# Attention scores in one transformer layer: cross terms over the whole array, high by high terms as pairs of 64-row tiles

## The reference

```python
def diff_attn_block(q, k, v, lam):
    s = jnp.einsum('bqhnd,bkhnd->bnhqk', q, k).astype(jnp.float32) * (1.0 / math.sqrt(HEAD_DIM))
    a = jax.nn.softmax(s, axis=-1)
    a = a[:, 0] - lam * a[:, 1]
    return jnp.einsum('bhqk,bkhv->bqhv', a.astype(v.dtype), v)
```

## Time and profile before

| what | us |
|---|---|
| median of 3 runs (3261.56 to 3263.18) | 3262.38 |
| the profiled execution, its own time | 3265.1 |
| its span, from first to last instruction | 3263.4 |
| TensorE busy in the span | 3125.3 |
| VectorE busy | 2255.1 |
| ScalarE busy | 1595.0 |

### The profile page before, as it was taken

The page is one execution under the profiler, slowest core; times in us unless marked ns, Lnnn a source line. Parts: engine busy times, 40 slices in busy tenths (PEclk is TensorE's granted clock), DMA queues, the critical chain, the costliest instruction groups (busy, mean ns, idle before and its releaser), DMA issues. The chain is left out here.

```text
span 3263.4 us, 67299 instructions
## 1 busy us (share of the span) xinstructions
PE 3125.3 (96%) x22654; PEld 2843.7 (87%) x22654; DVE 2255.1 (69%) x3873; ACT 1595.0 (49%) x3504; POOL 691.6 (21%) x894
## 2 busy tenths in 40 slices
PE   6999999999999999998989985999999999999998
PEld 4988989989998998997878874999999989998997
DVE  4888878878888888887974446555555555555564
ACT  4556656656666666665741123333333433333332
POOL 2532333333333233331310001111111111111111
PEclk8999999999999999999999986999999999999999
DMA  8654344344334345434325543655655555655664
GB/s 289 241 197 125 126 139 131 120 134 139 125 119 152 120 125 154 126 119 149 115 94 213 193 168 129 195 188 189 200 185 181 181 181 191 196 181 183 199 198 119
DMA packets 341095, 530.90 MB, mean 163 GB/s; under 512 B 29658, under 2 KB 256218, under 8 KB 325722
## 3 DMA queue, kind: packets, MB, share of 16 engines
q1 hardware_dynamic: 331228, 494.52, 46.4%
q0 software_dynamic: 9728, 34.61, 4.2%
HBM read 439.10 MB, written 89.16 MB: 162 GB/s over the span
## 5 line engine op out<-in xcount | busy, mean ns | idle before, releaser
L2749 PE MATMUL ps_gu<-xT,e_w 128*128 128x272 f32 x6144 | 782.9, 290 | 2.1 <-DVE xT L2909 2.1
L2749 PEld LDWEIGHTS ps_gu<-xT,e_w 128*128 128x128 f32 x6144 | 778.8, 189 | 4.0 <-issue 2.3
L2898 DVE TENSOR_TENSOR e_w<-e_raw,e_w 128x2048 fp32r<-128x2048 f32 x190 | 435.1, 2290 | 308.0 <-ACT e_w L2802 308.0
L1182 ACT ACTIVATE e<-ps_s,negm 128x1024 f32<-128x1024 f32 (+2 forms) x416 | 473.9, 1144 | 240.7 <-DVE negm L1583 200.2
L1568 DVE TENSOR_REDUCE mx<-ps_s 128x1 f32<-128x1024 f32 (+3 forms) x428 | 526.4, 1233 | 66.1 <-PE ps_s L821 62.0
L821 PE MATMUL ps_s<-kT,qT 128*128 128x512 f32 (+1 forms) x1920 | 478.5, 387 | 14.2 <-ACT e L1182 13.2
L2802 ACT CAST e_w<-e_raw 128x2048 fp32r<-128x2048 f32 x190 | 361.7, 1904 | 187.6 <-PE ps_d L2731 121.2
L821 PEld LDWEIGHTS ps_s<-kT,qT 128*128 128x128 f32 x1920 | 342.8, 191 | 85.8 <-ACT e L1182 28.7
L895 PE MATMUL ps_m<-w,hT 128*128 128x384 f32 x2040 | 392.4, 341 | 3.9 <-DVE o L1635 3.9
L863 PE MATMUL ps_m<-v,aT 128*128 128x128 f32 x2816 | 370.2, 279 | 1.3 <-ACT aT L1166 1.3
L895 PEld LDWEIGHTS ps_m<-w,hT 128*128 128x128 f32 x2040 | 349.7, 189 | 5.4 <-issue 5.4
(11 more groups left out here) (374 smaller groups left out, 3962.7 us busy)
## 6 DMA issues: line engine op xcount, KB each, us to landing
hT<-hT_d SPq DMA_DIRECT2D x85, 1024.0 KB, 5.4
e_raw<-w_gate SPq DMA_DIRECT2D x64, 1024.0 KB, 5.2
e_raw<-w_up SPq DMA_DIRECT2D x64, 1024.0 KB, 7.5
e_raw<-w_down SPq DMA_DIRECT2D x64, 1024.0 KB, 5.0
tab<-tabs_d SPq DMA_DIRECT2D x85, 256.0 KB, 2.7
hT_d<-hT SPq DMA_DIRECT2D x17, 1024.0 KB, 3.9
w_lent<-w_ada SPq DMA_DIRECT2D x16, 1024.0 KB, 5.5
cat_d<-cat_h SPq DMA_DIRECT2D x102, 128.0 KB, 4.7
```

What stands on the lines that cost most here:

```text
L1182: nc.scalar.activation(out, src, ACT.Exp, bias=negm[:, s.par, c:c + 1], scale=HD ** -0.5, accum_out=acc).then_inc(exp_done.sem, 1)
L2749: mm = nc.tensor.matmul(ps_gu[:, 2 * (s % 2) + f, 0:SLOTS], w_view(s, a)[:, k, f * P:f * P + P], xT[:, b, k, :], start=(k == 0 and a + b = ...
L2898: nc.vector.tensor_tensor(w[:, s % RING, 1, :], raw[:, s % RAW, :], w[:, s % RING, 0, :].bitcast(F32), ALU.subtract).then_inc(w_lo, 1)
```

## The change

Each unit of 1024 keys keeps its two banks of 512 columns but is computed otherwise. The key tiles (128 keys) of a unit alternate: even ones have the high parts in the upper 64 rows, odd ones now have the low parts there. The first bank holds the four even tiles, the second the four odd ones, so the moving operand is four runs of 128 columns. For each bank one matmul over the whole array makes both cross terms (half 1 for even tiles, half 0 for odd ones), and one matmul on 64 rows makes high by high: rows 0 to 63 for the first bank, rows 64 to 127 for the second. The low by low product is left out. The last 256 keys are computed as before. Since the columns of the scores are now in another order, `weighted` picks the value tiles through KEY_TILE. On swapped steps (tiles 2, 4, ... 14) `split_kq` and `low_kq` each become two instructions of half the width, and so do the copies of the cached keys. `turn(s, 0)` now stands ahead of the two 64-row matmuls of group 1.

```diff
+    KEY_TILE = [8 * (b // 8) + (2 * (b % 8) if b % 8 < 4 else 2 * (b % 8) - 7) if b < NS else b for b in range(BLOCKS)]
...
+        def swapped(s):
+
+            ref = s.i if s.j is None else s.first + s.odd
+            return 0 < ref < NS and ref % 2 == 0
...
+            def group_scores(s, c, n, lo, hi):
+
+                keys = kT[:, (s.h - 1) % 2, c]
+                q = [qT[:, s.par, (2 * half + c) * P:(2 * half + c + 1) * P] for half in range(2)]
+                paired = hi - lo >= 1024
+                if paired:
+                    tiles = keys[:, lo:lo + 1024].rearrange("p (b o n) -> p b o n", o=2, n=P)
+                    for odd in range(2):
+                        nc.tensor.matmul(ps_s[:, lo + 512 * odd:lo + 512 * odd + 512], q[1 - odd], tiles[:, :, odd, :],
+                                         start=True, stop=False)
+                if hi == KEYS:
+                    if paired and c == 0 and s.back == "prompt":
+                        weighted(s, 0)
+                    for half in range(2):
+                        mm = nc.tensor.matmul(ps_s[:, 2048:KEYS], q[half], keys[:, 2048:KEYS], start=(half == 0), stop=(half == 1))
+                if c == 0 and n == 1 and s.back == "sample" and not late(s):
+                    turn(s, 0)
+                if paired:
+                    for odd in range(2):
+                        rows = slice(64 * odd, 64 * odd + 64)
+                        mm = nc.tensor.matmul(ps_s[:, lo + 512 * odd:lo + 512 * odd + 512], q[odd][rows],
+                                              tiles[rows, :, odd, :], start=False, stop=True)
+                return mm
...
-                        for half in range(2):
-                            lhs = stationary[:, (2 * half + c) * P:(2 * half + c + 1) * P]
-                            for x in range(first, last, 512):
-                                y = min(x + 512, last)
-                                if c == 0 and n == 1 and half == 1 and x == first + 512 and s.back == "sample" and not late(s):
-                                    turn(s, 0)
-                                keys = kT[:, head % 2, c, x:y] if s.front == "sample" else kTp[:, head % 2, c, :]
-                                mm = nc.tensor.matmul(ps_s[:, at + x - lo:at + y - lo], lhs, keys, start=(half == 0),
-                                                      stop=(half == 1))
+                    else:
+                        mm = group_scores(s, c, n, lo, hi)
...
-                    vals = v[:, head % 2, b, :] if s.back == "sample" else vp[:, head % 2, :]
+                    vals = v[:, head % 2, KEY_TILE[b], :] if s.back == "sample" else vp[:, head % 2, :]
...
-                nc.scalar.copy(parts[:, :, 0, :].bitcast(F32R), rot[:]).then_inc(hi_done.sem, 1)
+                if swapped(s):
+                    nc.scalar.copy(parts[:, 0:2, 0, :].bitcast(F32R), rot[:, 0:2, :])
+                    nc.scalar.copy(parts[:, 2:4, 1, :].bitcast(F32R), rot[:, 2:4, :]).then_inc(hi_done.sem, 1)
+                else:
+                    nc.scalar.copy(parts[:, :, 0, :].bitcast(F32R), rot[:]).then_inc(hi_done.sem, 1)
...
-                nc.scalar.copy(past_parts[:, :, :, 0, :].bitcast(F32R), past[:]).then_inc(past_hi, 1)
+                nc.scalar.copy(past_parts[:, 0, :, 0, :].bitcast(F32R), past[:, 0])
+                nc.scalar.copy(past_parts[:, 1, :, 1, :].bitcast(F32R), past[:, 1]).then_inc(past_hi, 1)
...
+                if swapped(s):
+                    nc.gpsimd.tensor_tensor(parts[:, 0:2, 1, :].bitcast(F32R), rot[:, 0:2, :], parts[:, 0:2, 0, :], ALU.subtract)
+                    nc.gpsimd.tensor_tensor(parts[:, 2:4, 0, :].bitcast(F32R), rot[:, 2:4, :], parts[:, 2:4, 1, :],
+                                            ALU.subtract).then_inc(lo_done.sem, 1)
```

More of the change, by code:

```diff
@@ L805, in scores @@
                         weighted(s, 0)
[L806 to L813, removed]
-                        for half in range(2):
-                            lhs = stationary[:, (2 * half + c) * P:(2 * half + c + 1) * P]
-                            for x in range(first, last, 512):
-                                y = min(x + 512, last)
-                                if c == 0 and n == 1 and half == 1 and x == first + 512 and s.back == "sample" and not late(s):
-                                    turn(s, 0)
-                                keys = kT[:, head % 2, c, x:y] if s.front == "sample" else kTp[:, head % 2, c, :]
-                                mm = nc.tensor.matmul(ps_s[:, at + x - lo:at + y - lo], lhs, keys, start=(half == 0),
-                                                      stop=(half == 1))
+                    if s.front == "prompt":
+                        for half in range(2):
+                            q = qTp[:, head % 2, (2 * half + c) * P:(2 * half + c + 1) * P]
+                            mm = nc.tensor.matmul(ps_s[:, 1024 * c:1024 * c + P], q, kTp[:, head % 2, c, :], start=(half == 0),
+                                                  stop=(half == 1))
+                    else:
+                        mm = group_scores(s, c, n, lo, hi)
                     mm.then_inc(s_ready.sem, 1)
@@ L1460, in low_kq @@
                 kq_ready.wait(pool, s)
-                nc.gpsimd.tensor_tensor(parts[:, :, 1, :].bitcast(F32R), rot[:], parts[:, :, 0, :],
-                                        ALU.subtract).then_inc(lo_done.sem, 1)
+                if swapped(s):
+                    nc.gpsimd.tensor_tensor(parts[:, 0:2, 1, :].bitcast(F32R), rot[:, 0:2, :], parts[:, 0:2, 0, :], ALU.subtract)
+                    nc.gpsimd.tensor_tensor(parts[:, 2:4, 0, :].bitcast(F32R), rot[:, 2:4, :], parts[:, 2:4, 1, :],
+                                            ALU.subtract).then_inc(lo_done.sem, 1)
+                else:
+                    nc.gpsimd.tensor_tensor(parts[:, :, 1, :].bitcast(F32R), rot[:], parts[:, :, 0, :],
+                                            ALU.subtract).then_inc(lo_done.sem, 1)
             def rsqrt_rows(t):
@@ L1602, in past_low @@
                 dve.wait_ge(past_hi, s.h + 1)
-                nc.vector.tensor_tensor(past_parts[:, :, :, 1, :].bitcast(F32R), past[:],
-                                        past_parts[:, :, :, 0, :], ALU.subtract).then_inc(past_lo, 1)
+                nc.vector.tensor_tensor(past_parts[:, 0, :, 1, :].bitcast(F32R), past[:, 0],
+                                        past_parts[:, 0, :, 0, :], ALU.subtract)
+                nc.vector.tensor_tensor(past_parts[:, 1, :, 0, :].bitcast(F32R), past[:, 1],
+                                        past_parts[:, 1, :, 1, :], ALU.subtract).then_inc(past_lo, 1)
             def copy_past(s):
```

## The result

The changed kernel takes 3307.18 us (median of 4 runs, 3306.07 to 3309.92) against 3262.78 for the kernel before (median of 4). The ratio is 1.0132, with a 95% interval of 1.012 to 1.0144: 44 us slower. The profiled execution took 3306.07, its span 3304.4, 41.0 longer than that of before.

A forecast was written before the change was run, and what follows sets the result against it. TensorE was taken to bound heads 1 to 5. A net 0.19 us a unit gave 61 us there plus 6 in the last head, +67 on 3262.4: 3330 us, range 3250 to 3400 (about 8 in 10).

The forecast's parts named there:

- TensorE sets the pace in heads 1 to 5, the last head has room: TensorE busy 1238.67 of 1259 us in heads 1 to 5, so changes show fully; 194.39 of 210 in the last.
- half of 12 us: Last head: 64 units at 0.19 us add 12 us to TensorE, of which half, 6 us, shows.
- The pair shares one pass: Scores matmuls: two 64-row matmuls run side by side in 0.24 us, saving 0.22 us a unit.
- The border: Scores units: changing tile shape on the way in and out, with unhidden first loads, costs 0.42 us a unit.
- Strided keys and split copies at 0: Scores' moving operand in four runs, and halved copies on ScalarE and GpSimd on swapped steps: no added time, 0 us.
- Row pairs without a border: Rival: row tiles don't drain TensorE, each scores unit saves 0.22 us; 73 us less, 3189 us; chance 0.17.
- A pair that does not overlap: Rival: the 64-row matmuls take two passes in place of one; 81 us more, 3411 us; chance 0.07.
- That something cancels out: Rival: scores pairs run in sequence without border, or the border costs about 0.22 us; 3262 us; chance 0.10.
- The clock stayed at 1.00: Sign: TensorE's granted clock stays at 1.00 in heads 1 to 5; a drop to 1.2 GHz would exceed the range.
- the waits before the transposes of parts: Sign: waits for parts before turn_kq don't grow, with 0.28 us free there.
- the starts came as described: Sign: pair starts 0.3 us or more after whole-array work, second within 0.01, next whole-array matmul 0.3 or more later.
- VectorE's wait for 1024-column scores: Sign: VectorE's waits for scores, 59.7 us before, grow.

The follow-up runs named there:

- e1: The changed kernel with its high by high matmuls on all 128 rows again, low by low added back; 3266.07 us, ratio 1.0006.
- the doubled variant: Changed kernel with both 64-row matmuls on rows 0 to 63, each right behind its bank's whole-array matmul, four crossings a unit; 3550.13 us, ratio 1.0882.

## Why the prediction was right

The direction, the mechanism and the range were right; the forecast of 3330 was 23 us too high. Step by step:

*TensorE sets the pace in heads 1 to 5, the last head has room.* Right for the first: 41.0 us of added span all lie there. For the last head I took half of 12 us; about 2 showed, by the traces with and without pairs there. The room was larger than I made it. It is not endless: with one more pass a unit it gave up 17.5 us.

*The pair shares one pass.* Right: 0.24 taken, within 0.01 of one pass, and 77 us more when it can't.

*The border.* The mechanism is shown by doubling it. Its size was the term that was off. I charged 0.42 a unit; one more way in and out costs 0.38 by the two variants that differ in it alone. With the pass saved, 0.38 - 0.23 = 0.15 a unit in place of 0.19, 48 us in place of 61. The parts of it are also as the column tiles had them: after a whole-array matmul the next shape starts late by 0.10, and its first weights are not hidden, 0.10 longer records. I had read 0.13 from a run of twelve for the second; the first matmul of such a run, at 2628.56 in the trace of the kernel before, shows it directly, with a record of 0.50 and its successor 0.34 behind it, 0.11 over the pace. (In the earlier trace rows the 32 matmuls from 2626.71 on include the four from 2628.24 on, which is why seven sets, and not eight, lie between the two.)

*What is left.* 48 against the 41.0 measured: 7 us, 0.09 a step. The all-rows variant (e1) and the changed kernel have the same matmuls in the same order, so their traces can be compared start by start, up to the last transposes of parts (324 units start by then, four of them in the last head):

| where | times | distance of starts, all rows to pairs (medians, us) | sum, us |
|---|---|---|---|
| way in: the first 64-row matmul | 324 | 0.23 to 0.33 behind 512 columns, 0.12 to 0.21 behind 256, 0.03 to 0.20 behind transposes | +36 |
| the second matmul of the pair | 324 | 0.24 to 0.00 | -82 |
| way out: what follows the pair | 319 | 0.23 to 0.42 or 0.43 | +60 |
| the start after that | 310 | +0.11 where a scores matmul or a projection follows the pair, +0.05 where a transpose does | +26 |
| all else | | | -2 |

Together 38 us. (Behind transposes the all-rows kernel has its first matmul 0.03 after them and the second 0.31 after that; a pair's way in costs 0.09 there as elsewhere, and 6 us of the first two lines cancel.) So one way in and out costs 0.36 us in this kernel, and the pair saves its pass of 0.23. It is 0.36 and not 0.38 since on 75 units the way out leads into transposes, whose first record is longer by less, and since some of these starts had been waiting anyway. The first distance in a second call, 0.31 where 0.23 is the pace, is the same in both and has no part in it. The other 3 us of the 41 lie between the kernel before and the all-rows variant. These are sums of one execution each.

The Trainium skill's page "TensorEngine Tiling (Array Packing)", Key Properties, says that changing the mode drains the engine. The traces now agree for 64 x 128 too: where 0.23 is the pace, the changed kernel has 0.33 between starts on the way in and 0.43 on the way out, and the doubled variant 0.43 at each change.

*Strided keys and split copies at 0.* Right within 0 to 5 us; the median says 1.3, the trace some 3.

*The rivals.* Row pairs without a border: refuted by the 0.43. A pair that does not overlap: refuted. That something cancels out: refuted.

*What the profile would show.* The clock stayed at 1.00, the waits before the transposes of parts did not grow, and the starts came as described, 0.43 and not 0.3 behind the pair. One sign was wrong: VectorE's wait for 1024-column scores did not grow, 60.2 us against 59.7:

```profile
L1598 DVE TENSOR_REDUCE mx<-ps_s 128x1 f32<-128x1024 f32 x224 | 273.2, 1221 | 60.6 <-PE ps_s L799 60.2
```

VectorE's idle time went elsewhere, in part to its copies behind `turn_kq`, which wait for the transposes of parts. The views of L923 before and L943 after give those waits (us, times):

```profile
  DVE qT_out L1621: 6.9, 33
  DVE qT_out L1653: 23.9, 75
```

## What to carry to other kernels

Packing two half-height matmuls into one pass pays only if the passes saved between two changes of tile shape are worth more than the changes. Here a way in and out costs 0.38 us and one saved pass of 512 columns gives 0.23, so one pair at a time loses 0.15, and two pairs in a row gain 0.08. Price the border from any other tile shape that the trace already shows, by starts and by the length of the first record behind it. And before gathering such work into one place, look at what the old order covered: each of my gathered orders lost at least what it saved at the border, to a copy, an exponential or a maximum that came too late (and, as I take it, to the mix).

## What the runs showed of the hardware that I had not expected

The price is symmetric: where single matmuls alternate there is 0.43 between starts into and out of the 64-row shape. It is about the same for these row tiles as for the column tiles of the kernel before, behind which the first whole-array matmul has the same record of 0.50. The unhidden load is paid once a pair (the two starts stay 0.003 us apart), and a second pair in the same shape costs only 0.24. What I read as the load that is not hidden, 0.10, is as long for 64 rows as for 128: the records are 0.49 and 0.50. The Trainium skill's page "TensorE: Matmul & The Clock Gate", LDWEIGHTS, says that load time goes by columns and not by rows, 128 columns divided by 1.2 giving 0.107 us by its rule. What the unhidden load adds here, 0.10 to 0.11 for both heights, agrees; the load's own record, 0.18 us on 64 rows and 0.19 on 128, is longer.
